# Two halves of 256 tokens, with half 0's expert rows fetched beside half 1's weight blocks

## The reference, cut to what matters

```python
def token_block(args):                 # 128 tokens at a time
    xb, ib, gb = args                  # ib: 128 experts chosen for each token
    u = jnp.take(expert_u, ib, axis=0)
    act = jax.nn.gelu(jnp.einsum('td,tkd->tk', xb, u).astype(jnp.float32), approximate=False)
    vv = jnp.take(expert_v, ib, axis=0)
    return jnp.einsum('tk,tkd->td', (gb * act).astype(h.dtype), vv)
```

## Time and profile before

| | |
|---|---|
| median of 3 runs | 3259.67 us |
| the profiled execution | 3258.34 us, its span 3256.5 us |
| dense stages, up to the first gather | 1942 us |
| expert stage | 1314.5 us |
| PE / VectorE / ScalarE / GpSimd busy | 86% / 43% / 19% / 19% |
| HBM traffic | 680 MB, of it 542 MB on the gather queue |

### The profile page before, as it was taken

The page is one execution under the profiler, slowest core; times in us unless marked ns, Lnnn a source line. Parts: engine busy times, 40 slices in busy tenths (PEclk is TensorE's granted clock), DMA queues, the critical chain, the costliest instruction groups (busy, mean ns, idle before and its releaser), DMA issues.

```text
span 3256.5 us, 19994 instructions
## 1 busy us (share of the span) xinstructions
PE 2789.7 (86%) x6660; PEld 1230.2 (38%) x6660; DVE 1391.5 (43%) x2857; ACT 632.9 (19%) x1408; POOL 630.4 (19%) x577
## 2 busy tenths in 40 slices
PE   7999999998999998997958976777878777778787
PEld 3444444443444443442523442323323333333333
DVE  1135002521221101403472686666666666666664
ACT  1002111620111000102720121222222222222221
POOL 0000000000000000000000014454444444444452
PEclk9999999999999999998979998998998999999999
DMA  3221222102244322121001019999999999999996
GB/s 138 78 78 57 73 78 84 33 33 77 104 155 155 138 94 77 52 77 52 1 0 65 26 45 422 422 421 422 422 421 421 421 422 422 421 421 421 421 417 266
DMA packets 143252, 679.92 MB, mean 209 GB/s; under 512 B 10640, under 2 KB 10784, under 8 KB 77616
## 3 DMA queue, kind: packets, MB, share of 16 engines
q0 software_dynamic: 75344, 542.21, 40.3%
q1 hardware_dynamic: 67808, 136.45, 11.7%
HBM read 676.48 MB, written 2.14 MB: 208 GB/s over the span
## 4 chain that ended last, share of the span: by engine, by line
PE 59%; DMA 21%; DVE 13%; issue 3%; ACT 2%; POOL 1%; DVEq 0%; ACTq 0%; POOLq 0%
PE PS L345 40%; DMA slots<-in_expert_uv,experts 20%; PE PS L644 7%; DVE ring L1216 3%; PE PS L342 3%; PE PS L430 1%; POOL slots L327 1%; DVE rt L896 1%; PE PS L359 1%; PE PS L366 1%; PE PS L411 1%; DVE slots L1196 1%; DVE slots L1200 1%; DVE slots L1202 1%; DMA ring<-in_expert_uv,experts 1%
## 5 line engine op out<-in xcount | busy, mean ns | idle before, releaser
L345 PE MATMUL PS<-slots,ring 128*128 128x512 f32 x3008 | 1313.0, 597 | 65.1 <-DVE slots L1031 27.6
L345 PEld LDWEIGHTS PS<-slots,ring 128*128 128x128 f32 x3008 | 573.6, 192 | 781.7 <-issue 710.7
L644 PE MATMUL PS<-slots,toep 128*128 128x512 f32 x1280 | 614.5, 634 | 156.2 <-ACT toep L869 156.2
L1216 DVE CUSTOM_DVE_ANT_0 slots<-slots 128x1024 f32<-128x1024 f32 x320 | 393.3, 1229 | 399.0 <-DMA slots<-in_expert_uv,experts 398.6
L644 PE MATMUL PS<-ring,toep 128*128 128x512 f32 x768 | 386.1, 657 | 156.7 <-ACT toep L869 156.7
L327 POOL DMA_INDIRECT slots<-in_expert_uv,experts x320 | 393.6, 1230 | 363.9 <-PE PS L644 340.2
L644 PEld LDWEIGHTS PS<-slots,toep 128*128 128x128 f32 x1280 | 253.8, 202 | 512.2 <-issue 303.9
L327 POOL DMA_INDIRECT ring<-in_expert_uv,experts x192 | 215.0, 1120 | 529.5 <-PE PS L644 290.2
L644 PEld LDWEIGHTS PS<-ring,toep 128*128 128x128 f32 x768 | 155.2, 209 | 386.7 <-ACT toep L869 208.7
L1216 DVE CUSTOM_DVE_ANT_0 ring<-ring,slots 128x1024 f32<-128x1024 f32 x192 | 228.1, 1223 | 80.0 <-DMA ring<-in_expert_uv,experts 80.0
L862 ACT ACTIVATE acts<-dots 128x4 f32<-128x4 f32 x128 | 26.3, 205 | 1018.2 <-DVE dots L1216 1018.2
(11 more groups left out here) (201 smaller groups left out, 1803.6 us busy)
## 6 DMA issues: line engine op xcount, KB each, us to landing
ring<-in_w_in SPq DMA_DIRECT2D x19, 2048.0 KB, 8.2
ring<-in_w_ada SPq DMA_DIRECT2D x12, 2048.0 KB, 7.9
ring<-in_w_up SPq DMA_DIRECT2D x8, 2048.0 KB, 12.4
ring<-in_w_down SPq DMA_DIRECT2D x8, 2048.0 KB, 12.5
ring<-in_w_gate SPq DMA_DIRECT2D x4, 2048.0 KB, 8.1
ring<-in_w_out SPq DMA_DIRECT2D x4, 2048.0 KB, 7.9
ring<-in_w_q_peer SPq DMA_DIRECT2D x4, 2048.0 KB, 7.9
slots<-in_expert_uv,experts POOLq DMA_INDIRECT x320, 19.0
```

Of the source, the lines that this page charges most:

```text
L345: mm = pe.matmul(PS[:, t, :], w[:, t * P:(t + 1) * P], moving[:, k, :], start=first and k == 0, stop=last and k == KT - 1)
L644: mm = pe.matmul(PS[:, 2 * (tt % 2) + half, :], diag[:, s % 4, :], uv_ring[s % 16][:, D + 512 * half:D + 512 * half + 512], start=False, s ...
L1216: dve.tensor_tensor_reduce(out=u, in0=u, in1=h2_tok[:, s // NSLOT, :], scale=1.0, scalar=0.0, op0=ALU.mult, op1=ALU.add, accum_out=dots[:, ...
```

## The change

The tokens are split into half 0 and half 1 of 256. Half 0 goes through all stages up to its expert lists, then half 1 does. Weight blocks become 1024 x 256 (1 MB, laid out contiguously by the host), a ring of four, and every block except `ADA` is loaded and multiplied once for each half: 2 x 102 blocks, each 2 output tiles x 8 matmuls with 256 columns, plus 24 `ADA` blocks in half 0. Attention, stick-breaking and mLSTM run per half; half 1 sees half 0's keys and values, some of which are stored to DRAM and read back. x comes transposed from the host. Sigmoid and SiLU are written with tanh. Head norms take the reciprocal of all 8 tiles at once, in one tile `hroot`, spread by small matmuls.

The expert work is a generator on each engine. `TICKS` calls one step of it per weight block of half 1, save three (99 calls). A step on VectorE is: coefficients and accumulation of group g - 1, dots of group g. A group of half 0 has 2 slots, one of half 1 has 4. Even slots' second-table rows are multiplied by PE as before, odd slots' are accumulated by VectorE (`scalar_tensor_tensor`, 1024 wide, into `acc`). Half 0's slots have 6 buffers, half 1's have 16, and half 1's gathers start when all dense work is done. What is left of half 0's groups after half 1 runs on without weight blocks.

On SP's queue the Toeplitz loads of heads 0 and 1 stand ahead of the load of block `Q1` 0 and wait for `corner`, which VectorE sets after block `CP` 3; the other heads' stand ahead of `WO` 0.

```diff
-NRING = 3
+T, HALVES, TT = 256, 2, 2
+NRING = 4
+BW = 256
...
+SEQ = []
+for _hf in range(HALVES):
+    _run = plain_run(CG, XC, BG, GC, GA, CP, Q1, K1, V1, AP_, WO)
+    _ada = iter(plain_run(ADA) if _hf == 0 else [])
+    for _b in plain_run(UP, DN):
+        _run.append(_b)
+        _run.extend(x for x in [next(_ada, None)] if x)
+    _run += plain_run(Q2, K2, V2, VM, QKM, OM, WO2, PQ)
+    SEQ += [(_hf, kind, i) for kind, i in _run]
+NB = len(SEQ)
+NO = {b: n for n, b in enumerate(SEQ)}
...
+NS = 4 * NSLOT
+GROUPS = [(s, s + 2) for s in range(0, 2 * NSLOT, 2)] + [(s, s + 4) for s in range(2 * NSLOT, NS, 4)]
+NG = len(GROUPS)
+GROUP_OF = [g for g, (s0, s1) in enumerate(GROUPS) for _ in range(s0, s1)]
...
+def on_pe(s):
+    return s % 2 == 0
...
+NUV0, NUV1 = 6, 16
...
+    _r = _p % NUV0 if _p < CHANGE else (_p - CHANGE) % NUV1
...
+TICKS = [int(hf == 1 and (kind, i) not in ((WO, 3), (DN, 15), (WO2, 3))) for hf, kind, i in SEQ]
...
+            def toeplitz(hf, h):
+                g, w = NH1 * hf + h, T * (hf + 1)
+                if h >= 2:
+                    sp.wait_ge(s_biased, 2 * (g - 1))
+                else:
+                    sp.wait_ge(corner, 2 * hf + h + 1)
...
+                if (kind, i) == (Q1, 0):
+                    toeplitz(hf, 0)
+                    toeplitz(hf, 1)
+                if (kind, i) == (WO, 0):
+                    for h in range(2, NH1):
+                        toeplitz(hf, h)
...
-                sp.dma_start(ring[:, n % NRING, :, :], source(n)).then_inc(w_loaded[n % NRING], 16)
+                weights(n)
...
+            for p, e in enumerate(ENTRIES):
+                r = BUF[e]
+                if p == CHANGE:
+                    gp.wait_ge(tok_copy, 18)
+                    gp.wait_ge(top_done, 10 * 32)
+                    gp.wait_ge(tile_done, 2 * NB)
+                if BEFORE[e] is not None:
+                    consumed(gp, BEFORE[e])
+                if e >= 0:
+                    if e % TOPK == 0:
+                        gp.wait_ge(routed, e // TOPK + 1)
+                    gp.indirect_dma_start(UV[r], None, a["expert_uv_2"],
+                                          bass.IndirectOffsetOnAxis(ap=experts[:, e % 256:e % 256 + 1], axis=0))\
+                        .then_inc(uv_in[r], 16)
...
+            def expert_steps():
+                yield
+                for g in range(1, NG + 1):
+                    for s in range(*GROUPS[g - 1]):
+                        if on_pe(s):
+                            n = PE_NO[s]
+                            if s % NSLOT == 0 and s:
+                                pe.wait_ge(fin_a, 2 * (s // NSLOT) - 1)
+                            pe.wait_ge(uv_in[BUF[s]], 16 * TIMES[s])
+                            pe.wait_ge(diag_done, n + 1)
+                            ends = n + 1 == PE_NO[NSLOT * (s // NSLOT + 1)]
+                            for j in range(2):
+                                mm = pe.matmul(PS[:, 6 + j, :], diag[:, n % 4, :], UV[BUF[s]][:, D + 512 * j:D + 512 * j + 512],
+                                               start=s % NSLOT == 0, stop=ends, **LAX)
+                            mm.then_inc(moe_mm, 1)
+                    yield
+            experts_pe = expert_steps()
...
+                    if t == 0 and n:
+                        for _ in range(TICKS[n - 1]):
+                            next(experts_pe)
...
+            def expert_steps():
+                for g in range(NG + 1):
+                    if g:
+                        act.wait_ge(coef_done, g)
+                        for s in range(*GROUPS[g - 1]):
+                            if on_pe(s):
+                                n = PE_NO[s]
+                                if n >= 4:
+                                    act.wait_ge(moe_mm, n - 3)
+                                act.activation(diag[:, n % 4, :], ident[:, :], ACT.Copy, scale=coef[:, s % 16:s % 16 + 1])\
+                                    .then_inc(diag_done, 1)
+                    if g < NG:
+                        s0, s1 = GROUPS[g]
+                        act.wait_ge(dot_done, s1)
+                        if s0 >= 16:
+                            act.wait_ge(coef_done, GROUP_OF[s1 - 17] + 1)
...
+            def dot_products(g):
+                s0, s1 = GROUPS[g]
+                if s0 >= 16:
+                    dve.wait_ge(gelu_done, GROUP_OF[s1 - 17] + 1)
+                for s in range(s0, s1):
+                    u = UV[BUF[s]][:, 0:D]
+                    dve.wait_ge(uv_in[BUF[s]], 16 * TIMES[s])
+                    dve.tensor_tensor_reduce(out=u, in0=u, in1=H2[s // 256][:, s // NSLOT % 2, :], scale=1.0, scalar=0.0,
+                                             op0=ALU.mult, op1=ALU.add, accum_out=dots[:, s % 16:s % 16 + 1])\
+                        .then_inc(dot_done, 1)
+
...
+            def accumulate(g):
+                dve.wait_ge(coef_done, g + 1)
+                for s in range(*GROUPS[g]):
+                    if not on_pe(s):
+                        n = s - PE_NO[s]
+                        v, c = UV[BUF[s]][:, D:2 * D], coef[:, s % 16:s % 16 + 1]
+                        if s // NSLOT and n == (s // NSLOT) * NSLOT - PE_NO[s // NSLOT * NSLOT]:
+                            dve.wait_ge(fin_b, s // NSLOT)
+                        if n == (s // NSLOT) * NSLOT - PE_NO[s // NSLOT * NSLOT]:
+                            dve.tensor_scalar(acc[:, :], v, c, None, ALU.mult).then_inc(acc_done, 1)
+                        else:
+                            dve.wait_ge(acc_done, n)
+                            dve.scalar_tensor_tensor(acc[:, :], v, c, acc[:, :], ALU.mult, ALU.add).then_inc(acc_done, 1)
+
...
+            def expert_steps():
+                for g in range(NG + 1):
+                    if g in FINISH_AT:
+                        finish(FINISH_AT[g])
+                    if g:
+                        coefficients(g - 1)
+                        accumulate(g - 1)
+                    if g < NG:
+                        dot_products(g)
+                        s0 = GROUPS[g][0]
+                        if s0 % TOPK == 0 and s0 // TOPK not in ((15, 31) if EARLY else (31,)):
+                            routing(s0 // TOPK + 1)
+                    yield
...
+                    tick(hf, CP, i)
+                for b in range(2):
+                    dve.memset(toep[0:64, b, 0:64], NEG).then_inc(corner, 1)
+                only_ticks(hf, Q1)
...
+                rms_modulate(4 * hf + 2, 0, x)
+                only_ticks(hf, Q2, K2)
...
+                only_ticks(hf, QKM, OM)
+                for j in range(8):
+                    conv(j)
+                    if j:
+                        silu(j - 1)
...
+            half(0)
+            routing(0)
+            half(1)
```

More of the change, by code:

```diff
@@ L41 @@
 NCOLS = _at
[L44 to L52, removed]
@@ L190, in build @@
[L190 to L199, removed]
@@ L434, in _ @@
-            n_items = NH1 * TT
-            for i in range(3):
-                scores(i)
-            for i in range(n_items):
-                if i + 3 < n_items:
-                    scores(i + 3)
-                transposes(i)
-                if i and i % TT == 0:
-                    values(i // TT - 1)
-            values(NH1 - 1)
-            pe.wait_ge(y_done, NH1 // 2)
-            plain(AP_, 2, tiles(6))
-            pe.wait_ge(merged_done, 8)
-            plain(WO, 2, tiles(5))
-            rms(1)
@@ L881, in _ @@
+            act.wait_ge(consts, 20)
+            rms_squares(0, X[0], lambda k: act.wait_ge(x_loaded, 16))
+            act.wait_ge(halved, 1)
+            half(0)
+            gate_exps(0)
+            half(1)
+            assert ticked == [n for n in range(NB) if SEQ[n][1] != ADA]
+            if EARLY:
+                gate_exps(16)
+            for _ in experts_act:
+                pass
         @block.vector
         def _(dve):
-            def done(kind, i, t):
-                dve.wait_ge(tile_done, 4 * block_no(kind, i) + t + 1)
@@ L1238, in _ @@
-            dve.wait_ge(tok_copy, 18)
-            routing(0, first=True)
-            for g in range(4 * NITEM):
-                if g % 4 == 0 and g // 4 + 1 < NITEM:
-                    routing(g // 4 + 1)
-                for s in range(4 * g, 4 * g + 4):
-                    dot(s)
-                if g:
-                    coefficients(g - 1)
-                if g % (4 * PH) == 2 and g > 2:
-                    finish(g // (4 * PH) - 1)
-            coefficients(4 * NITEM - 1)
-            finish(TT - 1)
@@ new lines, in _ @@
+            dve.wait_ge(par_loaded, 16)
+            dve.tensor_scalar(half_b[:, :], par[:, COLS["b_gate"]:COLS["b_gate"] + 16], 0.5, None, ALU.mult).then_inc(halved, 1)
+            dve.wait_ge(consts, 20)
+            rms_inverse(0)
+            rms_scale(0, X[0], lambda k: col("norm1", k))
+            half(0)
+            routing(0)
+            half(1)
+            assert ticked == [n for n in range(NB) if SEQ[n][1] != ADA]
```

(5 more changed lines are left out.)

2103 lines of the change are left out of this document (1180 added, 923 removed).

## The result

| | before | after |
|---|---|---|
| median, us | 3259.32 | 3271.45 |
| range of the runs, us | 3258.76 to 3263.26 | 3268.32 to 3275.07 |
| profiled span, us | 3256.5 | 3266.5 |
| mean granted clock of PE | 0.942 | 0.859 |

The changed kernel takes 1.0035 times as long (interval 1.0022 to 1.0048): slower by 0.35%, where 6.4% faster was forecast. 220 us of span had to be found, 3266.5 against the 3046 of the sum.

The account below looks back on a forecast made before the run. PE was taken to bound the dense work and the DMA the expert work behind it; half 0 1007, half 1 1240 and the rest 799 sum to 3046 us of span, 3050 us as median, range 2970 to 3190.

Parts of the forecast that it names:

- The attention: Stage time scaled by tile widths, each head waiting for its values twice: 64 us in half 0, 88 in half 1.
- The left-over slots: Behind the dense work, half 0's 58 remaining slots go through six buffers at 5.05 us a pair: 146 us.
- `UP` and `DN`: Half 0's `UP` and `DN` blocks, 221 us, with 24 `ADA` parts at 0.4 us: 231 us.
- The steps: Half 1's blocks: each of 99 steps adds 1.72 us on PE, 170 in all; 10 us allowed for VectorE's load.
- rivals 1: Six buffers too few: gathers take 19.0 us, half 1's blocks with steps 11.7 us, whole 3360 us; chance 5%.
- Rival 2: Mixed weight and row traffic slower than gathers alone, 338 GB/s: blocks with steps 9.3 us, whole 3120 us; chance 15%.
- Rivals 3: Steps couple the engines, a late gather stopping the next block: 1.5 us a step, whole 3200 us; chance 10%.
- the queue behind `corner`: SP queues `Q1` 0's load behind Toeplitz loads awaiting `corner`: PE waits 10 us in half 0, 16 in half 1.
- the balance of the 99 steps: 198 slots save 492 us at the end; steps cost 170 + 10 + 17 + 17 in half 1: net 278 us.
- the convolution under the steps: Half 1's gate rows: with steps, 17 us of convolution no longer lie under PE's matmuls, 34 us for 17.
- 4: Weight loads show at 256 columns in all blocks: 0.11 us for 6528 records, 718 us, whole 3770 us; chance 1%.
- Rival 5: Half-wide narrow stages shrink by more than taken, 15% off some 640 us: whole 2955 us; chance 9%.

Follow-up runs that it names:

- experiment 7: Changed kernel with look-ahead of three, 16 buffers from slot 202, Toeplitz loads ahead of `Q1` 3 and the `ADA` sum ahead of the residual: 3057.06 us.
- experiment 5: Changed kernel with no expert step in any weight block and 16 buffers from slot 6 on: 3520.96 us.
- experiment 10: Kernel of experiment 7 with one in eight dealt slots on PE up to slot 182, one in two from there: 2983.98 us.
- experiment 1: Changed kernel with PE issuing attention scores three items ahead of the transposes instead of two, same three banks: 3130.44 us.

## Why the prediction was wrong

| Term of the sum, us | predicted | measured in after |
|---|---|---|
| Block; block with a step | 6.91; 8.63 | 6.91; 8.6 |
| Prologue, `CG` to `V1` of half 0 | 17 + 263 | 16 + 273 |
| Hole ahead of `Q1`, half 0; half 1 | 10; 16 | 9.2; 13.1 |
| **Attention, half 0; half 1** | **64; 88** | **116; 191.5** |
| `UP`, `DN` with `ADA` | 231 | 247.5 |
| `OM` to `WO2`, half 0; half 1 | 111; 157 | 110; 145.6 |
| `PQ` of half 1 | 93 | 96.5 |
| **58 left-over slots** | **146** | **174** |
| Groups of 4 slots at the end | 9.94 | 10.1, 10.2 with the tile changes |

Half 0 ended 60 us later than its sum, 52 of them in the attention; half 1 took 98 more, the attention 103; behind the dense work 62 were lost. Smaller errors cancel in part: the blocks `Q1` to `V1` took 107 us in half 0 and 128 in half 1 where the sum has 97 and 117 (no experiment looked at it), and the norm stretches of half 0 took 6.4 to 6.9 us where 8 or 9 were put.

- **The attention**, 155 of the 220 us. The step that failed is "Each head now waits for its values twice, once a half; half 0, with the narrow tiles, I put at 64 and half 1 at 88". It scaled the stage's time and went by the tile widths, and left out an edit of the same function: the look-ahead. With that edit put back the stage measures 72.4 and 87.2, so the term was within 9 us but for it. That it was scaled as a whole hid the question which wait in it ends last; no row of before stands in the prediction that shows when `scores` are issued against `transposes`. Among the signs named beforehand the attention stands only as a stretch with little DMA.
- **The left-over slots.** The failed step is "The 58 go through six buffers at 5.05 a pair": that is 1.6% over the DMA's 4.97 us for two slots, and puts nothing for a buffer that comes back late. In the blocks PE gives one back after 1.72 us of matmuls; in this stretch it is half idle and takes up to 3.75. Measured 6.0 a pair, and 5.15 with sixteen buffers. Another 9 us pass until slot 198, 12 more than a group's time from slot 256 to 260, and about 17 over the last 248 slots, at 10.2 a group with their tile changes for 9.94: there the DMA share is 1.00 and VectorE is busy for 520.71 of 610 us, so the DMA bounds it, at 414 GB/s for the 422 of the sum.
- **`UP` and `DN`.** The two pairs of long periods, 12.0 + 9.0 and 12.4 + 9.4 us for 7.4, were not seen: VectorE does the residual, which waits for the block's end, ahead of the `ADA` sum on which PE then waits. 13 us, shown by experiment 7.
- **The steps.** The start of half 1 has one stall of 10 us, block `CG` 2 with 18.3 us where without steps (experiment 5) it takes 6.9. PE waits there for its first diagonal matrix:

```profile
1081.76 1.23 DVE L1137 CUSTOM_DVE_ANT_0 uv<-uv,h_tok 128x1024 f32<-128x1024 f32 x1 [7.67 <-DMA uv<-in_expert_uv,experts]
...
1091.98 3.75 PE L442 MATMUL PS<-uv,diag 128*128 128x512 f32 x4 [7.32 <-ACT diag L826]
```

VectorE waits for the first gather, then does the next list (from 1085.40 us on) ahead of the coefficients (1091.24), and the four records take 3.75 us for 1.72. `BG` 2 and `DN` 7 lose 2.5 and 1.2 us more. That fills the 10 us that the prediction allowed the steps, but nearly all in the first one and not in every eighth, so that term came true in part by luck. PE waiting for a diagonal was named as a sign of rivals 1 to 3; it came in single blocks. The 1.72 us a step are right too, though 7.13 us of the earlier trace rows for 16 records give 1.78; 1.72 is four times 0.43.
- **What held.** The blocks, with and without steps; the queue behind `corner`; the balance of the 99 steps, 277.8 us for 278 by the medians and 283.4 by the spans; stick-breaking and lists. One term of that balance didn't hold: the convolution under the steps was to cost 17 us, and `OM` to `WO2` of half 1 takes 145.6 with steps and 140.3 without (experiment 5), so it cost 5. Rival 1 (six buffers) has no part in the blocks and 25 us in the left-over slots. Rival 2 has none: stretches with both kinds of transfer reach 399 GB/s. Rivals 3 and 4 fall with blocks of 6.91 and 8.6. Rival 5 got nothing: from `OM` to `WO2` half 0 took 110 us for 111, and half 1 without steps 140.3 for 140.
- **The chances.** Three rivals were about the new traffic, one about weight loads, one about narrow stages getting shorter; none gave a chance to a narrow stage getting longer by its hand-written order. The mechanism of the gain was right, and a version with the order put back is 4% faster, the tuned one 8.4%.

The Trainium skill, "TensorE: Matmul & The Clock Gate" (Parts 3 and 2), would charge every 128-column weight load, 107 ns each, to PE unless the row group differs. The first row of the window table does not agree: 641 records and their 640 loads fill 138.3 us, 6.91 us a block. The Trainium skill, "DMA: Bandwidth & Descriptors", section "Where 436 GB/s comes from", has about 358 GB/s for a core's loads from HBM; the last 610 us of after ran at 414 and the mixed stage of experiment 10 at 399, so here the measurement decides too.

## What to carry to other kernels

Where a stage is a hand-written pipeline over several engines, write down for each engine what stands behind what before you scale its time: one item less of look-ahead on one engine closed a loop with the order on another and doubled the stage, in this kernel and, alone, in the one before. When a change frees or takes a buffer or a PSUM bank, look at every look-ahead that used it, and at whether the shorter one was needed: here three banks carried a look-ahead of three. A step priced in a stage where an engine runs without pause costs more in a stage where it waits, so a buffer's return has to be priced there anew.

## What the runs showed of the hardware

In half 1's attention a chain of waits brought the low clock, and the low clock lengthened the chain: the stage had PE busy for 122.78 us at a granted clock of 0.63, and for 77.27 us at 0.96 when the loop was open. But a PE that is hardly idle doesn't always get the full clock: in half 0's attention of experiment 1 it was busy for 67.9 of 72.4 us and the clock stayed at 0.53, with matmuls of 128 and 256 columns in short pieces. From 320 us on it had no idle time in the record and stayed at the lower of the two levels (1.2 GHz):

```profile
320.00:340.00 20.00, 20.00 (x53) 10.36 (x51) 7.74 (x29) 10.81 (x38) 0.00 (x0) 0.50 0.16 30
```

Blocks of 256-column matmuls with a weight load each kept 1.00.
